# Transposed projections, a stationary v and one attention break per head pair in a hybrid encoder layer

## The reference, cut to what matters

```python
h = _rmsnorm(x, ln_g[l])
(qa, ka, va, za, qb, ckv, iq, ik, iw, zb, qc, kc, vc, zc, ga, gb, gc) = _split_cols(h @ w_in[l])
ckv = _rmsnorm(ckv, ckv_g[l])
ya = _mixer_a(qa, ka, va, sink[l], t5_bias) * jax.nn.silu(za)
yb = _mixer_b(qb, ckv, iq, ik, iw, w_uk[l], w_uv[l], t5_bias) * jax.nn.silu(zb)
yc = _mixer_c(qc, kc, vc, c_rel_bias[l]) * jax.nn.silu(zc)
merged = (jax.nn.sigmoid(ga) * (ya @ w_pa[l]) + jax.nn.sigmoid(gb) * (yb @ w_pb[l])
          + jax.nn.sigmoid(gc) * (yc @ w_pc[l]))
x = x + merged @ w_o[l]
return _rmsnorm(x, final_g)
```

## Time and profile before

| | |
|---|---|
| profiled execution, its own time | 1018.98 us |
| its span, first to last instruction | 1017.2 us |
| PE, matmuls | 1001.8 us busy, 98% |
| PE, weight loads (PEld) | 827.3 us, 81% |
| DVE / ACT / POOL | 573.2 / 469.8 / 101.3 us |
| mean DMA rate over the span | 184 GB/s |

### The profile page before, as it was taken

One profiled execution on the slowest core, in us unless ns is written; L12 is line 12 of the kernel. 1 busy time (PEld: TensorE's weight loads), 2 busy tenths in 40 slices (PEclk: granted clock), 3 DMA queues, 4 the chain that ended last, 5 costly groups with the idle time before them and its releaser, 6 DMA issues.

```text
span 1017.2 us, 14153 instructions
## 1 busy us (share of the span) xinstructions
PE 1001.8 (98%) x4835; PEld 827.3 (81%) x4835; DVE 573.2 (56%) x954; ACT 469.8 (46%) x757; POOL 101.3 (10%) x125
## 2 busy tenths in 40 slices
PE   8999999999999999999999999999999999999995
PEld 6887888888888888888888888888888888888884
DVE  6656555555655555655645557566456545545652
ACT  6554444444444445543544455445434434444441
POOL 1000211111110300221211002211000000000000
PEclk9999999999999999999999999999999999999998
DMA  9765555555555555555556555555455865555452
GB/s 307 243 207 172 172 180 187 169 173 160 164 175 175 176 166 176 188 174 175 161 184 182 166 176 187 169 174 164 156 195 166 316 220 188 189 181 186 166 197 92
DMA packets 106218, 187.01 MB, mean 184 GB/s; under 512 B 12752, under 2 KB 24096, under 8 KB 105536
## 3 DMA queue, kind: packets, MB, share of 16 engines
q1 hardware_dynamic: 105792, 186.21, 57.0%
q0 software_dynamic: 240, 0.24, 0.1%
q10 hardware_dynamic: 144, 0.01, 0.0%
HBM read 184.26 MB, written 2.17 MB: 183 GB/s over the span
## 4 chain that ended last, share of the span: by engine, by line
PE 97%; DMA 1%; DVE 0%; SPq 0%; issue 0%; ACT 0%; POOLq 0%; DVEq 0%; POOL 0%
PE bank L1010 29%; PE bank L1012 29%; PE bank L1011 28%; PE bank L984 4%; PE bank L1033 2%; PE bank L1147 1%; PE bank L1049 1%; PE bank L1050 1%; PE bank L1048 1%; DMA raw<-in_w_in_dram 1%; PE bank L1122 0%; SPq L329 0%; PE bank L1086 0%; PE bank L1085 0%; PE bank L1084 0%; DVE act L975 0%
## 5 line engine op out<-in xcount | busy, mean ns | idle before, releaser
L703 DVE TENSOR_TENSOR w_lo<-raw,w_hi 128x1024 fp32r<-128x1024 f32 (+1 forms) x324 | 400.8, 1252 | 279.9 <-ACT w_hi L502 278.5
L1010 PE MATMUL bank<-w_hi,h_hi 128*128 128x512 f32 x1088 | 436.0, 401 | 2.5 <-DVE w_lo L703 2.5
L502 ACT ACTIVATE w_hi<-raw 128x1024 fp32r<-128x1024 f32 (+1 forms) x324 | 336.0, 1050 | 209.2 <-PE bank L1012 190.6
L1012 PE MATMUL bank<-w_hi,h_lo 128*128 128x512 f32 x1088 | 425.0, 391 | 0.0
L1011 PE MATMUL bank<-w_lo,h_hi 128*128 128x512 f32 x1088 | 423.7, 389 | 0.0
L1010 PEld LDWEIGHTS bank<-w_hi,h_hi 128*128 128x128 f32 x1088 | 204.4, 188 | 44.6 <-issue 3.1
L1012 PEld LDWEIGHTS bank<-w_hi,h_lo 128*128 128x128 f32 x1088 | 204.2, 188 | 44.1
L1011 PEld LDWEIGHTS bank<-w_lo,h_hi 128*128 128x128 f32 x1088 | 204.7, 188 | 39.6
L438 POOL TENSOR_TENSOR biasmask<-bias,masks 128x512 f32<-128x512 f32 (+1 forms) x48 | 65.2, 1378 | 245.3 <-DMA bias<-bias_table 241.0
L1010 PE MATMUL bank<-w_hi,y_hi 128*128 128x512 f32 x192 | 76.4, 398 | 0.0
L1012 PE MATMUL bank<-w_hi,y_lo 128*128 128x512 f32 x192 | 75.0, 390 | 0.0
(11 more groups left out here) (152 smaller groups left out, 578.8 us busy)
## 6 DMA issues: line engine op xcount, KB each, us to landing
raw<-in_w_in_dram SPq DMA_DIRECT2D x232, 512.0 KB, 4.3
raw<-in_w_o_dram SPq DMA_DIRECT2D x32, 512.0 KB, 4.2
raw<-in_w_pa_dram SPq DMA_DIRECT2D x16, 512.0 KB, 3.6
raw<-in_w_pb_dram SPq DMA_DIRECT2D x16, 512.0 KB, 3.6
raw<-in_w_pc_dram SPq DMA_DIRECT2D x16, 512.0 KB, 4.5
bias<-bias_table SPq DMA_DIRECT2D x24, 256.0 KB, 4.9
raw<-in_w_in_dram SPq DMA_DIRECT2D x16, 256.0 KB, 5.9
act<-in_x_t_dram SPq DMA_DIRECT2D x8, 256.0 KB, 6.4
```

Of the source, the lines that this page charges most:

```text
L502: nc.scalar.activation(w_hi[:, s, 0:n], raw[:, s, 0:n], ACT.Copy).then_inc(hi_ready, 1)
L703: nc.vector.tensor_tensor(w_lo[:, s, 0:n], raw[:, s, 0:n], w_hi[:, s, 0:n].bitcast(F32), ALU.subtract).then_inc(lo_ready, 1)
L1010: mm(acc, xh, wh[:, e, :], start=first, stop=False)
L1012: ins = mm(acc, xl, wh[:, e, :], start=False, stop=last)
```

## The change

The kernel is written again around the same three-matmul products:

- q, k of C, the index queries and the path z are projected transposed: now 128 columns of weights are stationary and the 256 rows of h moving (`cols_step`). q and k come out as the scores need them, the gated result as P needs it. Chunks of q, k and z are quarters (4 pieces, 256 columns).
- v is stationary in the product with the exponentials: 64 columns of v, 128 moving columns of `probsT`, each head into 64 partitions of a bank. The exponentials are divided by their sum before (POOL, L412), and the result is multiplied with the SiLU path by DVE.
- One break of the stream per pair: slot i holds the product with v of pair i-1, the scores of pair i+1 and the transposes of pair i.
- k and v of B come from ckv in hi and lo parts, as chunks `uk` and `uv` of the stream, for all pairs together.
- Since a transposed result has the sequence in its columns, 1/rms is now a row: the squares of x are summed by POOL (3 adds of 128 x 1024 and two smaller ones) and PE, POOL takes the power on 128 x 256 values, and multiplies x with it in 4 steps of 128 x 1024; ACT and DVE then split h again.
- The host lays out all weights in the order of use (`w_s`, one contiguous block of rows per piece) and full bias tables with the masks in them (`bias`). The loops are unrolled.

```diff
+CHUNKS = ([("kvc", 0, 0), ("iq", 0, 0), ("ik", 0, 0)] + quarters("q", 0) + quarters("z", 0)
+          + [k for u in range(4) for k in (("q", 1, u), ("uk", 0, u))]
+          + [("q", 2, 0), ("uv", 0, 0), ("q", 2, 1), ("uv", 0, 1), ("q", 2, 2), ("q", 2, 3)]
+          + quarters("k", 0) + [("v", 0, 0), ("v", 0, 1)] + quarters("z", 1)
+          + branch(0) + quarters("z", 2) + branch(1) + branch(2) + quarters("o", 0))
...
+            def load(g):
+                s, n = g % RING, width(g)
+                wait(sp, lo_ready, g - RING + 1)
+                sp.dma_start(raw[:, s, 0:n], w_s[g, :, 0:n]).then_inc(raw_in[s], 16)
...
+            pool.wait_ge(row_mean, 1)
+            nc.gpsimd.tensor_tensor(rstd_row[:, :], mean_row[:, :], neg_half[:, :], ALU.pow).then_inc(row_rstd, 1)
+            pool.wait_ge(row_mean, 2)
+            nc.gpsimd.tensor_tensor(rstd[:, 0, :], mean_sq[:, 0, :], neg_half[:, 0:NT], ALU.pow
+                                    ).then_inc(rstd_ready, 1)
...
+            for k in range(4):
+                xs = x_cols(4 * k, 4).rearrange("p (k s) -> p k s", k=4)
+                nc.gpsimd.tensor_tensor(xs, xs, rstd_row[:, :].unsqueeze(1).to_broadcast([P, 4, SEQ]), ALU.mult
+                                        ).then_inc(x_scaled, 1)
...
+                for h in range(2):
+                    for t in (1, 0):
+                        s = scores[:, h, t_of(t)]
+                        nc.gpsimd.tensor_scalar(s, s, r_denom[:, h, t:t + 1], None, ALU.mult).then_inc(norm_ready, 1)
...
+            def hT_group(k):
+                sc.wait_ge(x_scaled, k + 1)
+                for kt in range(4 * k, 4 * k + 4):
+                    nc.scalar.activation(h_hi[:, kt, :], x_cols(kt), ACT.Copy, scale=ln_gT[:, kt:kt + 1]
+                                         ).then_inc(hT_hi, 1)
...
+            def cols_step(g, c, e, kt, n_kt, hi_t, lo_t):
+                n_blk = 4 if KINDS[c] == "iq" else 2
+                wh, wl = parts(g, n_blk * P)
+                for n in range(n_blk):
+                    cols = slice(n * P, (n + 1) * P)
+                    acc = bank[2 * (c % 2) + n][:, 0:SEQ]
+                    mm(acc, wh[:, e, cols], hi_t[:, kt, :], start=kt == 0, stop=False)
+                    mm(acc, wh[:, e, cols], lo_t[:, kt, :], start=False, stop=False)
+                    ins = mm(acc, wl[:, e, cols], hi_t[:, kt, :], start=False, stop=kt == n_kt - 1)
...
-                        o1 = bank[4][:, P + HD * h:P + HD * (h + 1)]
-                        mm(o1, probsT[:, h, 0:P], v_cols(br, m, 0, h), start=True, stop=False)
-                        mm(o1, probsT[:, h, P:2 * P], v_cols(br, m, 1, h), start=False, stop=True)
...
+                    for blk, t, kt, first, last in ((0, 1, 0, True, False), (1, 1, 1, False, True),
+                                                    (2, 0, 0, True, True)):
+                        for h in range(2):
+                            ins = mm(bank[4 + t][HD * h:HD * (h + 1), SROW:CH], v_cols(p, kt, h),
+                                     probsT[:, h, blk * P:(blk + 1) * P], start=first, stop=last)
```

More of the change, by code:

```diff
@@ L92, in bucket, with hybrid_trunk @@
     return 24 + log_bucket(rel - 1, 8, 4, 64) if rel > 0 else log_bucket(-rel, 24, 12, 128)
[L95 to L109, removed]
+def hybrid_trunk(nc, x, x_t, w_s, bias, ckv_g, sink, final_g, out):
     x_v = x[0].rearrange("(t p) n -> p t n", p=P)
     out_v = out[0].rearrange("(t p) n -> p t n", p=P)
-    ZCOL = [COL["za"], COL["zb"], COL["zc"]]
-    GCOL = [COL["ga"], COL["gb"], COL["gc"]]
     with ExitStack() as ctx:
@@ L483, in _ @@
-            for br in (1, 2):
-                for u in range(2):
-                    stage(br, Idx(u))
-                with pool.Fori(0, 3) as i:
-                    for u in range(2):
-                        stage(br, Idx(2 + u, 2, i))
-            rms(2, ssq_f[:, :], D, 4)
+            nc.gpsimd.memset(causal[0:HD, 3 * HD:4 * HD], NEG).then_inc(mask_ready, 1)
+            nc.gpsimd.memset(causal[0:HD, 5 * HD:6 * HD], NEG).then_inc(mask_ready, 1)
+            pool.wait_ge(sq_x, 2)
+            nc.gpsimd.tensor_tensor(squares[:, 0:1024], squares[:, 0:1024], squares[:, 1024:2048], ALU.add
+                                    ).then_inc(sq_sum, 1)
@@ L553, in _ @@
-            for j in range(8):
-                hi(Idx(FIRST[1] + j + LEAD))
-                if 1 <= j <= 4:
-                    t, half = (j - 1) // 2, (j - 1) % 2
-                    sc.wait_ge(x_in[t], 16)
-                    part = x_rows[:, t, D // 2 * half:D // 2 * (half + 1)]
-                    nc.scalar.activation(part, part, ACT.Square, accum_out=ssq_x[:, t, half:half + 1]
-                                         ).then_inc(sq_x, 1)
-            sc.wait_ge(used, FIRST[1])
-            sc.wait_ge(rstd_ready, 1)
@@ L757, in hT_group @@
+            def hT_group(k):
+                ve.wait_ge(used, FIRST[AT["ik", 0, 0]] + k + 1)
+                for kt in range(4 * k, 4 * k + 4):
                     ve.wait_ge(hT_hi, kt + 1)
@@ new lines, in silu_chunk, with merge_chunk @@
+            def silu_chunk(c):
+                _, b, u = CHUNKS[c]
+                wait(ve, y_ready, 2 * 8 * b)
+                for half in range(2):
+                    ve.wait_ge(tanh_ready, tanhs_before(c) + half + 1)
+                    ins = nc.vector.scalar_tensor_tensor(
+                        silu[:, 2 * u + half, :], gate[:, half, 0:SEQ], 1.0, bank[2 * (c % 2) + half][:, 0:SEQ],
+                        ALU.add, ALU.mult)
+                ins.then_inc(dve_evac, 1)
+            def merge_chunk(c):
+                _, b, n = CHUNKS[c]
+                ve.wait_ge(used, FIRST[c + 1])
+                ve.wait_ge(tanh_ready, tanhs_before(c))
+                for t in range(NT):
+                    dst = merged_v[:, t, CH * n:CH * (n + 1)]
+                    acc = bank[2 * (c % 2) + t][:, :]
```

1489 lines of the change are left out of this document (699 added, 790 removed).

## The result

The changed kernel takes 1043.10 us (median of 4 runs, 1042.41 to 1043.89), the kernel before 1018.59 in the same session. The ratio is 1.024, with a 95% interval of 1.0222 to 1.0258: slower by 24.5 us, where 26 us less were forecast. 1043 lies outside the range of 979 to 1012. The mechanism is that of rival C, whose price was 1054.

The account below looks back on a forecast made before the run. PE was taken as the bound, waiting for nobody in the long middle. Changed PE work plus new waits, +9.7 - 4.9 - 29.6 - 5.9 + 0.1 - 2.5 + 7 = -26.1 us, took 1018.6 to 993 us, range 979 to 1012.

Parts of the forecast that it names:

- rival C: POOL's power costs 0.26 us a column, PE stands still some 60 us: 1054 us; chance 8%.
- 6: Row of 1/rms: PE waits for the chain of power, multiplications and splits; +7 us (2 to 68), power T = 5.
- Step 1: Transposed projections: 1440 products of 512 columns become 2880 of 256 at 0.1167 us each; +9.7 us.
- Step 3: Pairs: q and k transposes go, v's heads run together (0.75 us), a slot is 2.41 us; net -29.6 us.
- Rival B: Product with v: its two heads run one after another, +13 us, 1006 us; chance 22%.
- Step 2: k and v of B: breaks and w_uk transposes go (15.9 us), 256- and 512-column matmuls come; net -4.9 us.
- Step 4: Transposes of y go, -5.9 us; other transposes and sums of squares on PE together +0.1 us.
- Step 5: Start: split first piece, 4 KB weight rows, thirteen warm-up matmuls, PE free near 7.1; -2.5 us (0 to -4).
- Step 7: Costed at nothing: DVE's sums, bias tables, copies, and POOL's four normalisations (1.5 to 2.7 us, 5.4 before their slot).
- A: Cheap end: 256 columns cost exactly half of 512 and the power's T is small: 979 us; chance 15%.
- D: Weight loads bind the 256-column matmuls at 0.187 us each, +209 us: 1202 us; chance 2%.
- E: No change within 0.2% (2 us), several of the other rivals half true; chance 2%.

Follow-up runs that it names:

- e1: Changed kernel with POOL's power on 128 x 2 values only, spread into a row by a DVE diagonal and a PE product with ones: 1007.46 us.
- e2: Changed kernel with powers of 2 to 256 columns and multiplications of 2 and 256 added on POOL behind the last pair: 1044.05 us, one run.
- e5: e1 without the scaling of x and second split of h; 1/rms applied as q, k, z, v and g leave their banks: 1003.58 us.
- e7: e1 with q, k and z projected by half as many products of 512 moving columns, so they hold other sums: 989.96 us.
- e3: e1 with the six products of one v head before the six of the other: 1014.39 us.
- e6: e5 with the squares added by DVE in iq instead of by POOL: 999.30 us.
- e9: e6 with hi and lo of h joined into products of 512 columns only in q of A and C, k and z: 994.64 us.
- e11: Changed kernel with 156 unread products of 512 columns ahead of PE's wait before the index keys: 1043.58 us.

## Why the prediction was wrong

**The step that failed is 6, the row of 1/rms,** with its choice "I take 0.02 a column, T = 5 us". T is 42.2 us, 0.16 a column. The step's two ends (2 to 68) hold what was measured, and so does rival C's condition, 0.12 a column or more; C's own 0.26 was too high, and so its 1054. The choice between the ends leant on the wrong row. An addition of 512 columns shows what POOL pays for moving data; it says nothing of what a power needs for each value. The row nearest in kind was the power on two columns, and a start of 0.7 us was an assumption that rows alone did not favour. The stage was given +7; it cost 42.0 less the 1.3 of iq's narrow products and the 0.9 of the sums on PE, about 40. e1 gives 35.6 of it back, and e2 shows the price by width. Rival C had 8%; between a start and a price for each column, with nothing to decide, I would now give a third.

Within that step the chain behind the power was rightly seen to bind even at T = 0 (1 to 3 us expected; 5 measured by taking it away in e1 to e5). POOL's multiplications took less than I had allowed, 2.47 us for 1024 columns and not 2.9. What I missed is that DVE's operations wait for them, which stretches `w_lo` of 288 columns from 0.45 to 2.6 us, and that the clock can fall behind PE's stops.

**Step 1 was mis-sized.** I took 0.1167 us from the products with 72 stationary columns. With 128 they stand 0.120 apart: 2880 x 0.120 - 326.4 = +19.2, not +9.7. e7 confirms the price from the other side. Of the two rows of before one had 128 columns but zeros, the other real data but 72 columns; the measured distance lies above both.

**Step 3 was right in its mechanism and 2 us off in size.** The two heads run together, the product with v is 0.80 us, not 0.75, and a slot is 2.50, not 2.41: 24 x 2.50 + 0.2 - 87.6 = -27.4, where -29.6 was forecast. Rival B did not come: one after another, at the 0.109 us that each row of starts keeps, 12 instructions would take 1.31. Its price of +13 was not measured; e3 shifts the heads by half of it and costs 6.9.

**Step 2** stands: four uk chunks of 1.44 and two uv of 2.75 us are 11.3, and 11.0 was forecast. **Step 4** has no sign against it: with the measured sizes the terms behind the first q make 2688 x 0.120 - 1344 x 0.2267 = +17.9, -27.4, -4.6, -5.9, -0.4 for the other transposes, and +1.6 for two small waits (0.66 us in the first q chunk, 0.90 in a slot), together -18.8, where -18.7 is measured.

**Step 5 was half right.** The first product came at 7.15 (near 7.1 forecast, 9.00 before). But to the end of kvc the start lost 1.3 us instead of gaining 2.5: POOL's additions hold up DVE's w_lo, PE stops for 2.4 us at 29, and behind it the clock's fall takes 1.5 more. What POOL's additions do to DVE I had costed in no term at all; e6 puts it at 4.3 us.

**Step 7** held but for one slot: at 782.83 PE waits 0.90 us for POOL, whose four normalisations took 5.76 us there, over the 5.4 that the step named as its cover. In the mean they took 4.5 (65.0 and 43.5 us in 24 pairs), where the step had 1.5 to 2.7: the cover was much thinner than it said. Rivals A, D and E are refuted: half the price for half the columns did not show, and 0.120 leaves no room for a weight load of 0.187.

Left open: why, behind the same stop at 29 us, the clock fell in seven executions and not in two; why the joined pair needs 0.352 and not 0.347; and whether e9's last stops (one in a slot, one in z, 2.1 us together) can be taken away.

## What to carry to other kernels

An operation's price has a part for each element that depends on the function; take it from a row of the same function, and where that row has only two columns, give the price per column as much weight as the price per instruction. If one rival's price is more than twice the forecast's whole gain (61 us against 26), a cheap way round (here a product with a diagonal) is worth more than the estimate. And a slow clock behind a wait has a price only where nothing else is late: fill the wait, and look whether the end moves, or look whether anything waits behind the slow products.

## What the runs showed of the hardware that I had not expected

- POOL's power costs 0.16 us for each column of 128 values, 55 times its multiplication: 41.24 against 0.74 us for 256 columns. It does not hold DVE up (e2: 28 `w_lo` beside it, median 1.22 us).
- POOL's additions and multiplications hold DVE up. A DVE operation with two inputs in SBUF of 0.44 us took 2.4 to 2.7 beside POOL's addition of 1024 columns, and one of 288 columns 2.6 beside its multiplication (the two of 91.71 us in the changed kernel). One with a single input in SBUF was held up too: L801 on 128 x 48 values took 1.20 us there and the same operation 0.18 in e1. Operations whose first input was in PSUM kept their 0.41 to 0.48 us. The Trainium skill, SBUF — State Buffer, section SBUF: two separate sides, calls the shared port pair "an exclusive lock, not a bandwidth split" for a DVE operation with two SBUF inputs against a GpSimd one that reads SBUF. By that rule the one that comes second waits for the whole of the other. For POOL's additions the traces agree in both directions: DVE's 2.43 to 2.68 us are the addition's 2.4 and little more, and POOL's additions of 512 and 256 columns took 2.14 and 1.59 us, each begun 1.0 us before DVE finished a `w_lo`, while a multiplication of 256 columns took 0.74 in e2. For the power they do not, and there the measurement decides: it left DVE alone for 41 us.
- A product costs more than its columns: 0.120 us for 256, 0.2267 for 512 with 128 stationary columns, so as if each paid 0.0133 beside 0.2133 for 512.
- After the same stop of PE at 29 us the granted clock fell in some executions and stayed in others (0.50 in the changed kernel, 1.00 in e1), and where it fell PE lost 1.5 us.
- At one and the same time, 1043, the mean granted clock was 0.974 in the changed kernel and 0.994 in e11.
